# Two heads at a time in two of four attentions, and three sets of column sums turned in later stages

## What is computed

```python
def first_block(x, ...):
    for layer in range(2):
        x = x + 0.5 * swiglu(rmsnorm(x, g[0]), w_in[layer, 0], w_out[layer, 0])     # ffn0, ffn2
        x = x + (even_mixer if layer == 0 else odd_mixer)(rmsnorm(x, g[1]), ...)
        x = x + 0.5 * swiglu(rmsnorm(x, g[2]), w_in[layer, 1], w_out[layer, 1])     # ffn1, ffn3
    return rmsnorm(x, final_norm_g)

# even_mixer: gated linear attention (4 heads, "GLA") beside "fox" attention, 8 heads of 64:
    s = q @ k.T * 64 ** -0.5 + (F[:, None] - F[None, :])      # F: running sum of log gates
    s = where(key <= query, s, -inf);  o = softmax(s) @ v
# odd_mixer: 16 heads of 64 on a shared latent c, keys picked by an index score (top 64):
    s = q_lat @ c_sel.T * 64 ** -0.5 + t5_bias;  o = softmax(masked s) @ c_sel

def second_block(x, c, ...):
    for l in range(2):
        ada = silu(c) @ w_ada[l] + b_ada[l]                   # 6 x 1024 numbers: shifts, scales, gates
        sh1, sc1, gt1, sh2, sc2, gt2 = split(ada, 6)
        y = mixer(x * (1 + sc1) + sh1, ...)                   # mix0, mix1: attention of 8 heads + convolution
        x = layer_norm(ALPHA * x + (1 + gt1) * y, ...)
        h = relu((x * (1 + sc2) + sh2) @ w_up[l]) ** 2 @ w_down[l]
        x = layer_norm(ALPHA * x + (1 + gt2) * h, ...)
```

## Time and profile before

| | us |
|---|---|
| median of 3 runs | 2018.8 (2013.42 to 2020.34) |
| the profiled execution | 2024.51 |
| its span | 2022.6 |
| TensorE busy | 1897.2 |
| VectorE busy | 1416.0 |
| ScalarE busy | 958.8 |
| GpSimd busy | 833.7 |

### The profile page before, as it was taken

One profiled execution on the slowest core, in us unless ns is written; L12 is line 12 of the kernel. 1 busy time (PEld: TensorE's weight loads), 2 busy tenths in 40 slices (PEclk: granted clock), 3 DMA queues, 4 the chain that ended last, 5 costly groups with the idle time before them and its releaser, 6 DMA issues.

```text
span 2022.6 us, 28189 instructions
## 1 busy us (share of the span) xinstructions
PE 1897.2 (94%) x11324; PEld 1655.3 (82%) x11324; DVE 1416.0 (70%) x1502; ACT 958.8 (47%) x1182; POOL 833.7 (41%) x392
## 2 busy tenths in 40 slices
PE   6899999999999999989999989998999899889997
PEld 5788896788888888865878879887888798888886
DVE  6987545399958885455699747966864579668743
ACT  5454363354444543334445434764643346646532
POOL 5967100097658775012386765950000049500000
PEclk8999897899999999985999979999999899999998
DMA  7777352267776876530477734434555344345550
GB/s 237 250 244 250 119 157 84 87 217 236 229 250 199 257 232 210 157 123 1 154 239 251 238 121 160 137 111 135 175 189 180 122 153 140 104 146 169 195 183 35
DMA packets 346548, 347.75 MB, mean 172 GB/s; under 512 B 15124, under 2 KB 341576, under 8 KB 346440
## 3 DMA queue, kind: packets, MB, share of 16 engines
q1 hardware_dynamic: 346408, 346.18, 53.3%
q10 hardware_dynamic: 32, 0.02, 0.0%
HBM read 345.11 MB, written 1.07 MB: 171 GB/s over the span
## 4 chain that ended last, share of the span: by engine, by line
PE 44%; issue 30%; POOL 12%; DVE 9%; ACT 2%; DMA 1%; SPq 1%; POOLq 1%; DVEq 0%; ACTq 0%
PE bank L855 19%; PE bank L854 10%; POOL arena L777 4%; POOL arena L743 4%; DVE wl L1644 3%; POOL arena L740 3%; PE bank L798 2%; PE bank L799 2%; PE bank L800 2%; PE bank L972 1%; DVE hx L1709 1%; PE bank L843 1%; ACT wh L1274 1%; PE bank L1172 1%; PE bank L995 1%
## 5 line engine op out<-in xcount | busy, mean ns | idle before, releaser
L1644 DVE TENSOR_TENSOR wl<-raw,wh 128x2048 fp32r<-128x2048 f32 (+1 forms) x279 | 755.0, 2707 | 327.3 <-ACT wh L1274 326.9
L855 PE MATMUL bank<-xx,wh 128*128 128x512 f32 x1920 | 682.4, 399 | 0.0
L1274 ACT ACTIVATE wh<-raw 128x2048 fp32r<-128x2048 f32 (+1 forms) x279 | 526.0, 1885 | 253.8 <-PE bank L855 194.1
L854 PE MATMUL bank<-xx,wl 128*128 128x256 f32 x1920 | 546.1, 284 | 45.1 <-DVE arena L1700 19.4
L855 PEld LDWEIGHTS bank<-xx,wh 128*128 128x128 f32 x1920 | 365.9, 191 | 84.1
L855 PE MATMUL bank<-hx,wh 128*128 128x512 f32 x1216 | 427.6, 395 | 0.0
L854 PEld LDWEIGHTS bank<-xx,wl 128*128 128x128 f32 x1920 | 368.7, 192 | 53.0 <-issue 48.3
L740 POOL TENSOR_TENSOR arena<-arena,csil 128x2048 f32<-128x2048 f32 x48 | 222.9, 4643 | 415.5 <-DVE xx L1655 221.0
L798 PE MATMUL bank<-xx,wh 128*128 128x256 f32 x1136 | 332.9, 293 | 14.1 <-DVE xx L1951 5.3
L854 PE MATMUL bank<-hx,wl 128*128 128x256 f32 x1216 | 345.0, 284 | 0.0
L799 PE MATMUL bank<-xx,wh 128*128 128x256 f32 x1136 | 327.4, 288 | 0.0
(11 more groups left out here) (262 smaller groups left out, 1991.4 us busy)
## 6 DMA issues: line engine op xcount, KB each, us to landing
raw<-in_ffn_w_in SPq DMA_DIRECT2D x88, 1024.0 KB, 5.2
arena<-in_w_ada SPq DMA_DIRECT2D x48, 1024.0 KB, 7.8
raw<-in_w_in SPq DMA_DIRECT2D x36, 1024.0 KB, 5.0
raw<-in_ffn_w_out SPq DMA_DIRECT2D x32, 1024.0 KB, 5.7
raw<-in_w_up SPq DMA_DIRECT2D x32, 1024.0 KB, 5.4
raw<-in_w_down SPq DMA_DIRECT2D x32, 1024.0 KB, 5.1
raw<-in_ffn_w_out SPq DMA_DIRECT2D x16, 768.0 KB, 6.6
raw<-in_even_w_in SPq DMA_DIRECT2D x12, 1024.0 KB, 5.3
```

Of the source, the lines that this page charges most:

```text
L854: pe.matmul(o[:, 0:T], lo_w, halves[:, 0, :], start=start, stop=False, skip_group_check=True)
L855: return pe.matmul(o.rearrange("p (h t) -> p h t", h=2), hi_w, halves, start=False, stop=stop, skip_group_check=True)
L1274: act.activation(wh[:, c % RING, at], raw[:, c % RING, at], ACT.Copy).then_inc(hi_made.sem, 1)
L1644: dve.tensor_tensor(wl[:, c % RING, at], raw[:, c % RING, at], wh[:, c % RING, at].bitcast(F32), ALU.subtract).then_inc(lo_made.sem, 1)
```

## The change

- `pe_pairs`, `act_pairs`, `dve_pairs` take the place of the attention functions in the even and the odd mixer. They go by pairs of heads. TensorE: scores of pair i, a block of both heads before the next block, into four banks; transposes of pair i-1; outputs of pair i-2, both heads' first blocks and then both heads' second blocks. VectorE: scaling of pair i-1, then minima of pair i, then the low half of pair i-3. `ns`, `pr`, `pt`, `nm`, `rs`, `ri` and `bm` have four buffers each. To make room, the arena's attention part grows to 12 x 384 columns, and `bm` and the mask `dm` lie where wukT was, so that VectorE waits for the keys before it makes the mask. The mix stages keep their functions, on buffers with new names.
- The 48 matmuls of `pe_ada` and `dve_ada` for ffn0 move from rms1 into the even mixer (TensorE: ahead of the GLA outputs, VectorE: at the halves), those for ffn2 from rms4 into the odd mixer (TensorE: ahead of "index", VectorE: ahead of the mask), those for ffn3 from the final norm (and mod0a) to just ahead of the attention of mix0. They write columns 256 and up of bank 0 or 7. Those for ffn1 stay in rms3. Waits for `ada_made` go, and some for `ada_summed` are added.

```diff
-ATT = 7 * 384
+ATT = 12 * 384
+    ADA_BANK = {"ffn0": 0, "ffn1": 7, "ffn2": 7, "ffn3": 0}
+    SCORES = (4, 5, 2, 3)
...
                 if n == 4:
                     sp.wait_ge(bias_stored.sem, 16)
+                    sp.wait_ge(ada_summed.sem, ada_summed.at("ffn2"))
                     sp.dma_start(bias8, src).then_inc(bias_loaded.sem, 16)
                 if n == 5:
-                    sp.wait_ge(ada_made.sem, ada_made.at("ffn2"))
...
+        def pe_pairs(s):
+            def scores(p):
+                if p >= 2:
+                    pe.wait_ge(ns_made.sem, ns_made.at(s, 2 * p - 2))
+                for at, qt, kt in ((slice(0, P), slice(0, P), slice(0, P)), (slice(P, 384), slice(P, T), slice(0, T))):
+                    for h in (2 * p, 2 * p + 1):
+                        last = pe.matmul(bank[SCORES[h % 4]][:, at], q(h)[:, qt], k(h)[:, kt], start=True, stop=not fox)
+                        if at.start > 0 and not fox:
+                            last.then_inc(score_made.sem, 1)
+                    if fox:
+                        for h in (2 * p, 2 * p + 1):
+                            last = pe.matmul(bank[SCORES[h % 4]][:, at], sel[32:40, h, :], fsum[32:40, kt], start=False, stop=True)
...
+            def output(p):
+                pe.wait_ge(pt_out.sem, pt_out.at(s, 2 * p + 2))
+                if p >= 2:
+                    pe.wait_ge(xl_made.sem, xl_made.at(s, XL_FIRST[s] + p - 1))
+                for h in (2 * p, 2 * p + 1):
+                    pe.matmul(b[half(h), 0:T], v(h, 0), pt[:, h % 4, 0:T], start=True, stop=False)
+                for h in (2 * p, 2 * p + 1):
+                    pe.matmul(b[half(h), P:T], v(h, 1), pt[:, h % 4, T:384], start=False, stop=True).then_inc(pv_made.sem, 1)
+            for i in range(pairs + 2):
+                if i < pairs:
+                    scores(i)
+                if 1 <= i <= pairs:
+                    transposes(2 * i - 2)
+                    transposes(2 * i - 1)
+                if i >= 2:
+                    output(i - 2)
...
+        def act_pairs(s):
+            for i in range(pairs + 2):
+                if i < pairs:
+                    exps(2 * i)
+                    exps(2 * i + 1)
+                if 1 <= i <= pairs:
+                    evacuate(2 * i - 2)
+                    evacuate(2 * i - 1)
+                if i >= 2:
+                    upper(i - 2)
...
+        def dve_pairs(s):
+            for i in range(pairs + 3):
+                if 1 <= i <= pairs:
+                    normalise(2 * i - 2)
+                    normalise(2 * i - 1)
+                if i < pairs:
+                    masked(2 * i)
+                    masked(2 * i + 1)
+                if i >= 3:
+                    rest(i - 3)
...
@@ in pe_even @@
             def outputs():
+                pe_ada("ffn0")
                 pe.wait_ge(gla_dve.sem, G_DVE["state"])
...
-            pe_attention(s)
+            pe_pairs(s)
...
@@ in pe_odd @@
             def index():
+                pe_ada("ffn2")
...
         def pe_ada(s):
-                last = pe.matmul(bank[7][:, n:n + 1], ...
+                last = pe.matmul(bank[at][:, T + n:T + n + 1], ...
...
@@ in pe_mix @@
             pe.wait_ge(rope_dve.sem, rope_dve.at(s))
+            if s == "mix0":
+                pe_ada("ffn3")
             pe_attention(s, ...)
...
                 pe_rms(s)
-                if before in ADA_OF:
+                if before == "ffn1":
                     pe_ada(before)
...
@@ in the program of VectorE @@
             def halves():
+                dve_ada("ffn0")
...
             def mask():
+                dve_ada("ffn2")
+                dve.wait_ge(mla_pe.sem, M_PE["K3"])
...
+            if s == "mix0":
+                dve_ada("ffn3")
+                dve_fold(1)
             dve_attention(s, meanwhile)
...
-                if s == "mod0a":
-                    dve_ada("ffn3")
-                    dve_fold(1)
```

More of the change, by code:

```diff
@@ L205, in build @@
     c = Carver(ARENA - ATT)
-    ns = c.take(2 * 384, "p (b k) -> p b k", b=2)
-    pr = c.take(3 * 384, "p (b k) -> p b k", b=3)
-    pt = c.take(2 * 384, "p (b k) -> p b k", b=2)
+    ns, pr, pt = (c.take(4 * 384, "p (b k) -> p b k", b=4) for _ in range(3))
     c = Carver(7 * 512)
@@ L1006, in pe_attention, with transposes @@
                     output(i - 3)
+        def pe_pairs(s):
+            pairs = heads_of[s] // 2
+            q, k, v, _ = att_of(s)
+            fox = s == "even"
+            pe.wait_ge(proj_out.sem, proj_out.at(s))
+            def scores(p):
[9 more added lines that the diff above has]
+                            last = pe.matmul(bank[SCORES[h % 4]][:, at], sel[32:40, h, :], fsum[32:40, kt], start=False, stop=True)
+                            if at.start > 0:
+                                last.then_inc(score_made.sem, 1)
+            def transposes(h):
+                pe.wait_ge(pn_made.sem, pn_made.at(s, h + 1))
+                if h >= 2:
+                    pe.wait_ge(pt_out.sem, pt_out.at(s, h - 1))
+                for j in range(3):
+                    at = slice(j * P, (j + 1) * P)
+                    last = pe.transpose(bank[6 + h % 2][:, at], pr[:, h % 4, at], ident[:, :])
+                last.then_inc(pt_made.sem, 1)
+            def output(p):
+                pe.wait_ge(pt_out.sem, pt_out.at(s, 2 * p + 2))
+                if p >= 2:
+                    pe.wait_ge(xl_made.sem, xl_made.at(s, XL_FIRST[s] + p - 1))
+                b = bank[p % 2]
+                for h in (2 * p, 2 * p + 1):
[10 more added lines that the diff above has]
+                    output(i - 2)
         def pe_even(s, moving):
@@ L1525, in act_odd @@
                     todo[step]()
[L1526 removed]
+            act_pairs(s)
             for j in range(3):
@@ L1780, in dve_attention, with masked, normalise, rest @@
                     rest((i - 4) // 2)
+        def dve_pairs(s):
+            pairs = heads_of[s] // 2
+            mask = att_of(s)[3]
+            def masked(h):
+                dve.wait_ge(score_made.sem, score_made.at(s, h + 1))
+                if s == "odd":
+                    dve.wait_ge(bm_made.sem, h + 1)
+                if h >= 4:
+                    dve.wait_ge(p_made.sem, p_made.at(s, h - 3))
+                for b, at in enumerate((slice(0, P), slice(P, 384))):
+                    last = dve.tensor_tensor_reduce(ns[:, h % 4, at], bank[SCORES[h % 4]][:, at], mask(h)[:, at], -SCALE, 3e38,
+                                                    ALU.add, ALU.min, nm[:, h % 4, b:b + 1])
+                last.then_inc(ns_made.sem, 1)
+            def normalise(h):
+                dve.wait_ge(p_made.sem, p_made.at(s, h + 1))
+                link(dve.reciprocal(ri[:, h % 4, :], rs[:, h % 4, :]))
+                for b, at in enumerate((slice(0, P), slice(P, 384))):
+                    last = dve.tensor_scalar(pr[:, h % 4, at], pr[:, h % 4, at], ri[:, h % 4, b:b + 1], None, ALU.mult)
+                last.then_inc(pn_made.sem, 1)
+            def rest(p):
+                i = XL_FIRST[s] + p
+                dve.wait_ge(xh_made.sem, xh_made.at(s, i + 1))
+                t = X_TILE[s] + p
+                dve.tensor_tensor(xl[:, t, :], bank[p % 2][:, 0:T], xh[:, t, :].bitcast(F32), ALU.subtract).then_inc(xl_made.sem, 1)
+            for i in range(pairs + 3):
[7 more added lines that the diff above has]
+                    rest(i - 3)
         def dve_out(s, c0):
@@ L2092, in _ @@
                 dve_rms(s)
-                if before in ADA_OF and s != "final":
+                if before == "ffn1":
                     dve_ada(before)
```

88 lines of the change are left out of this document (56 added, 32 removed).

## The result

The changed kernel takes **1989.2 us** (median of 4 runs, 1984.3 to 1992.5), against 2019.6 us before (4 runs): ratio 0.984, 95% interval 0.981 to 0.986 (the two medians alone give 0.985), 30 us less. The prediction was 2000 us, in a range of 1977 to 2015. The profiled execution took 1984.3 us (span 1982.5), 5 us under its median, and that of before 2024.5 us, 5 us over. Between the two profiles there are thus 40 us to account for, and some 10 of them are spread among executions. The rows count instructions, two for each of these float32 products and one for a transpose: the "eight matmuls" of the prediction are four, and the 48 of a set of sums are 24 products of one column each.

A forecast was written before the change was run, and what follows sets the result against it. TensorE, busy 94% of the span and mostly at the low clock in both attentions, was taken as the bound. Terms -6 +14.5 -14 -1.5 -22 +9.8 = -19.2 us from 2018.8 gave about 2000 us, range 1977 to 2015.

The forecast's parts named there:

- slower rival: Attentions: two heads' products don't overlap in the steady state, pairs save nothing, only the sums count: +16.8, 2036 us; chance 0.07.
- Even attention: Even mixer's attention by pairs, 8.2 us a pair at the low clock: 32 us, 14 less (bounds 9 and 18).
- four pairs 32.8, less 3: Even attention: four pairs' TensorE time, 32.8 us, less 3 for scores that still start at the full clock.
- Odd attention: Odd mixer's attention by pairs, eight pairs of 4.2 us: 41 us, 22 less (bounds 14 and 26).
- ring rival: Attentions: the VectorE and ScalarE loop sets the pair, odd 5.3 us, even 9.5; total -5, 2014 us; chance 0.13.
- First norm: Norm after ffn0: without its sums, the small products can start some 6 us earlier: -6 (bounds -4 and -7).
- The sums ahead of the GLA outputs: Even mixer: ffn0's sums cost 7, then outputs and next chunk run partly at low clock: +14.5 (bounds +5.5 and +19).
- The rival in which the clock holds: All moved sums: clock holds through them, about 5.2 us each; sum -34, 1985 us; chance 0.2.
- Norm after ffn2: Odd mixer: ffn2's sums moved behind the first chunk's turns, cover 7.2 us: net -1.5 (bounds -5 and +4).
- the sums, and the index products behind them at the low clock, want 10: Odd mixer, after ffn2: TensorE time the moved sums and index products need, 10 us, against 7.2 us of cover.
- Last norm and mix0: ffn3's sums: removal from the last norm gives 0, return before mix0's attention costs +9.8 (bounds +4.5 and +11).

The follow-up runs named there:

- kernel with products apart: Changed kernel with buffers and other engines' order kept, but TensorE issues each head's scores and outputs whole before the other's: 2027.8 us, ratio 1.004 to the kernel before.
- minima first: Changed kernel with VectorE's minima of a pair queued ahead of the scaling of the pair before: 2011.2 us, ratio 0.995 to the kernel before.
- pairs only: Changed kernel with all three turned sums back in the norm stages, leaving the attention by pairs: 1978.5 us, ratio 0.980 to the kernel before.
- sums-only kernel: Changed kernel with attention by single heads as before, leaving only the three moved sums: 2036.6 us, ratio 1.009 to the kernel before.
- spread kernel: Changed kernel with ffn0's sums dealt out, six instructions behind each of the even mixer's chunks 1 to 8: 1980.0 us, ratio 0.979 to the kernel before.
- the two couples that isolate it: Pairs with only ffn2's sums moved against pairs with none moved: 1977.8 against 1978.5 us; both with GpSimd's bias adds later: 1969.1 against 1974.9 us.

## Why the prediction was right, and where its sizes were off

**Bound and direction** held: the gain is TensorE's in the attentions, and the kernel with products apart shows that the two heads' overlap carries it. In the prediction this rested on the single row of 0.93 us. The slower rival (no overlap in the steady state) is refuted by the 0.93 and 1.65 us for eight score instructions.

**Even attention**: 14 less was said, 17.3 came. The pair at the low clock was right (8.2 said, 7.98 measured), the scores too (5.1 said, 340.22 to 345.25 is 5.03). The term that was mis-sized is "four pairs 32.8, less 3": TensorE was busy for 27.6 us, not 29.8. The first scores gained less from the full clock than said (3.69 us in place of 5.03), but the clock rose once more at 348.2, and the last pair's scores took 3.04 us in place of 5.03. Idle time and end were said to be 2.4 us, and TensorE was idle for 0.6.

**Odd attention**: 22 less was said, 28.4 came. The step that failed is the choice of 4.2 us between VectorE's 3.8 and TensorE's 4.7 at the low clock. The clock rose, TensorE dropped out as the bound, and the pair sits at VectorE's end, 3.68 us. The estimate of that end from the rows of before was good, one head held up by the adds and the other free. With 3.68 the sum would still give 36.9: eight pairs have seven intervals (25.2 us), and start and end took 7.0 and 2.3. The Trainium skill, "TensorE: Matmul & The Clock Gate", Part 4, says that transposes don't count as busy in the same way and that the full clock doesn't engage for them; the prediction weighed this as a clock that stays down, with 4.7 us a pair. The trace disagrees, the stretch had 0.95. The Trainium skill, the same page, Part 1 ("What's actually happening"), says that the clock is set by how busy the engine was recently. If that is read as the profile's busy share, the trace disagrees too: 0.54 at 93% before, 0.95 at 65% after. The ring rival's mechanism thus came true in part: in the odd mixer VectorE's work is the bound, but at 3.68 and not at 5.3 us. The order that the change gives VectorE keeps it short (minima first: 7.41).

**First norm**: -6 was said; the small products start at 226.67 in place of 232.68 us, and the chunk behind them ends 7.0 us earlier, as the first low clock is shorter too.

**The sums ahead of the GLA outputs**: +14.5 was said. Measured: 5.6 for the sums, and 6.0 for what is behind them up to the GLA norm's end (19.4 us in the changed kernel, 13.4 in pairs only), 11.6 in all, or 13 as the sums-only kernel has it. The block lets the clock fall, as said, near its end, and the spread kernel shows that the fall costs about as much as the sums themselves. Over all of A the forecast was +8.5 (-6 and +14.5), and the profiles have +3.0. The rival in which the clock holds is refuted for the block, and met by the spread.

**Norm after ffn2**: -1.5 was said; C is 7.1 us shorter in the changed kernel and 3.4 and 4.1 us in the two couples that isolate it. "The sums, and the index products behind them at the low clock, want 10" was mis-sized: the sums took 5.4 to 7.6 us, and the keys' wait fell from 4.54 to 0.94 us.

**Last norm and mix0**: 0 and +9.8 were said. The sums in mix0 took 10.37 us, at 0.50, and putting them back takes 12.3 us out of E and 8 out of the median. Right, and the one part of the change that should simply be undone.

**Sum**: in the two profiles the attentions gave 45.7 us where 36 was said, and all the rest cost 5.6 where 16.8 was said; that is 40 us, of which 10 are the distance of the two profiled executions from their medians. In the medians the moved sums cost 10 to 17.7 us, near the 16.8. So most of the 11 us between the 2000 said and the 1989 measured is the attentions' 9.7.

## What to carry to other kernels

Put products that use different rows or different columns of the array next to each other in the queue, and put a ring's oldest step (here the scaling) ahead of its youngest on every engine; the first halves the time of such products, and the second kept an odd pair at 3.68 us where the other order had up to 7.41, with a lower clock. Before moving small work out of a stage, see what hides it there; if it must go into a dense stream, deal it out in small portions and not in one block (A: 86.0 us in place of 93.7). Where GpSimd and VectorE share a loop, let GpSimd's adds run beside VectorE's reads from PSUM; here it took 1 to 2 us off the stage.

## What was not expected of the hardware

- TensorE's clock stood higher with less work: 0.95 over 34.6 us with the engine busy for 65% in side-by-side products, 0.56 over 61.4 us with the same products apart and 91% busy (55.8 us).
- 48 one-column instructions cost 5.6 us at the full clock and 10.4 at the low one. In one block they were followed by 13.7 to 17 us of low clock (297.6 to 311.3 us in the changed kernel, 300.0 to 317.0 in sums only); in eight portions by none.
- With minima first, TensorE's wait in a pair grew from 0.81 to 2.51 us and the pair from 3.68 to 7.41: more than half of the difference was work at the low clock. Which of the two brings the other isn't shown.
- VectorE's scaling of 256 columns took 347 ns alone and 827 ns beside a GpSimd add, and its minima 419 ns in both cases.
